# Keys turned in 32x32 blocks by VectorE, and the plain transfers issued by SyncE, in a hybrid mLSTM / gMLP / memory-attention layer with a hierarchical MoE

## The reference

```python
mem_k = (rmsnorm(mem_prompt) @ w_k)        # prompt: 256 memory tokens, 4 heads of 256; also an output
# sample: the keys come from cache_mem_k (256 tokens, 4 heads of 256)
z = rmsnorm(x) @ w_in                      # ONE projection: mLSTM q,k,v,o,i,f; gMLP u,v; memory queries mq; gates
qm = mq_raw.reshape(B, L, MEM_HEADS, MEM_HEAD_DIM)
sc = jnp.einsum('blhd,bmhd->bhlm', qm, mem_k).astype(f32) * (MEM_HEAD_DIM ** -0.5)
a = jax.nn.softmax(sc, axis=-1).astype(x.dtype)
att = jnp.einsum('bhlm,bmhd->blhd', a, mem_v).reshape(B, L, MEM_WIDTH)
# then three gated branches, w_out, the MoE (32 experts), the final norm
```

## Time and profile before

| | |
|---|---|
| median of 3 runs | 845.39 us (845.02 to 845.53) |
| the profiled execution, its own time | 845.18 us |
| its span in the trace | 843.4 us |
| granted TensorE clock, as a share of full speed | 0.995 |
| busy share of PE, DVE, ACT, POOL | 98%, 70%, 56%, 11% |

### The profile page before, as it was taken

One profiled execution on the slowest core, in us unless ns is written; L12 is line 12 of the kernel. 1 busy time (PEld: TensorE's weight loads), 2 busy tenths in 40 slices (PEclk: granted clock), 3 DMA queues, 4 the chain that ended last, 5 costly groups with the idle time before them and its releaser, 6 DMA issues. The chain is left out here.

```text
span 843.4 us, 12205 instructions
## 1 busy us (share of the span) xinstructions
PE 826.6 (98%) x4776; PEld 735.4 (87%) x4776; DVE 588.2 (70%) x820; ACT 469.7 (56%) x622; POOL 94.3 (11%) x163
## 2 busy tenths in 40 slices
PE   7999999999999999999999999999999999999994
PEld 7979999988989998899999999878888888888883
DVE  5665487773455457695565556778889989889893
ACT  5655487753433234554334336656868768677763
POOL 3103101040010010000000010010004102210410
PEclk9999999999999999999999999999999999999998
DMA  9658533335543436345436457579999999999960
GB/s 283 211 174 295 166 113 113 113 118 158 184 138 128 161 125 192 120 151 162 148 110 217 150 207 249 207 264 409 395 358 348 363 391 381 357 353 406 363 247 18
DMA packets 96097, 190.78 MB, mean 226 GB/s; under 512 B 5892, under 2 KB 60448, under 8 KB 95904
## 3 DMA queue, kind: packets, MB, share of 16 engines
q1 hardware_dynamic: 90288, 172.52, 58.9%
q0 software_dynamic: 4944, 15.75, 5.4%
q10 hardware_dynamic: 800, 1.66, 0.6%
HBM read 180.65 MB, written 10.03 MB: 226 GB/s over the span
## 5 line engine op out<-in xcount | busy, mean ns | idle before, releaser
L1492 DVE TENSOR_TENSOR w_r<-arena,w_r 128x2048 fp32r<-128x2048 f32 x96 | 216.9, 2285 | 27.7 <-ACT w_r L1088 27.7
L1483 DVE TENSOR_TENSOR unit_r<-arena,unit_r 128x2048 fp32r<-128x2048 f32 x63 | 145.0, 2302 | 128.7 <-ACT unit_r L1077 128.6
L632 PE MATMUL pj<-xn_r,unit_r 128*128 128x320 f32 x1536 | 233.9, 311 | 0.0
L632 PEld LDWEIGHTS pj<-xn_r,unit_r 128*128 128x128 f32 x1536 | 225.6, 188 | 3.7 <-issue 3.0
L979 PE MATMUL pj<-w_r,xg 128*128 128x512 f32 x768 | 191.0, 398 | 0.5 <-DVE xg L1476 0.4
L1088 ACT ACTIVATE w_r<-arena 128x2048 fp32r<-128x2048 f32 x96 | 180.4, 1910 | 2.9 <-DMA arena<-in_w_exp_down 2.1
L979 PEld LDWEIGHTS pj<-w_r,xg 128*128 128x128 f32 x768 | 141.8, 188 | 31.4 <-DVE xg L1476 0.8
L1077 ACT ACTIVATE unit_r<-arena 128x2048 fp32r<-128x2048 f32 x63 | 120.2, 1908 | 42.3 <-PE pj L632 23.6
L1008 PE MATMUL pj<-w_r,hidT 128*128 128x512 f32 x384 | 93.3, 392 | 0.6 <-ACT hidT L1339 0.6
L1008 PEld LDWEIGHTS pj<-w_r,hidT 128*128 128x128 f32 x384 | 71.8, 188 | 17.0 <-issue 0.8
L632 PE MATMUL pj<-br_r,unit_r 128*128 128x320 f32 x384 | 59.6, 311 | 0.0
(11 more groups left out here) (375 smaller groups left out, 834.0 us busy)
## 6 DMA issues: line engine op xcount, KB each, us to landing
arena<-in_w_in SPq DMA_DIRECT2D x40, 1024.0 KB, 5.3
arena<-in_w_exp_gate SPq DMA_DIRECT2D x64, 512.0 KB, 4.7
arena<-in_w_exp_up SPq DMA_DIRECT2D x64, 512.0 KB, 6.5
arena<-in_w_exp_down SPq DMA_DIRECT2D x64, 512.0 KB, 5.6
arena<-in_w_mem_v SPq DMA_DIRECT2D x4, 1024.0 KB, 5.2
arena<-in_w_br_mem SPq DMA_DIRECT2D x4, 1024.0 KB, 4.9
arena<-in_w_br_mlstm SPq DMA_DIRECT2D x4, 1024.0 KB, 5.0
arena<-in_w_br_gmlp SPq DMA_DIRECT2D x4, 1024.0 KB, 5.0
```

What stands on the lines that cost most here:

```text
L632: last = mm(bank_of(s)[0:out_rows, 0:out_cols], l, r, start=k == 0, stop=k == len(pairs) - 1)
L1483: v.tensor_tensor(unit_r[n % RING][:, 1, :], raw_unit[unit_slot(n)], unit_r[n % RING][:, 0, :], ALU.subtract).then_inc(u_lo, 1)
L1492: v.tensor_tensor(w_r[u % NS][:, 1, :], raw_w[u % NS], w_r[u % NS][:, 0, :], ALU.subtract).then_inc(m_lo, 1)
```

## The change

Keys. Each head's keys are loaded in a form in which transposing 32x32 blocks is the whole turn: partition 32a + i, place (b, j, t) holds key 32b + i, dim 64a + 2j + t. It takes four transfers of 32 partitions for each head and source, each run of 64 floats (256 bytes). The prompt's keys are read back for this from the output `mem_k_prompt`, once it is written. DVE's 32x32 transpose (`v.transpose`, two for each head) writes `kmT` directly; PE's eight `ka` steps and their PSUM banks are gone. A key dim then stands at partition 32a + j, half t, so the query columns must be in the same order: for the units of `mq`, ACT and DVE read the raw unit with a step of two floats and write even columns, then odd columns (`turned`, `unit_part`, `raw_columns`).

Transfers. All that POOL issued, other than the indirect gathers and scatters, is now issued by SP, between the unit loads. Each stands behind a named unit's load.

```diff
-    ka = lambda h: (step("ka", h, 0), step("ka", h, 1))
+    ka = lambda h: (step("ka", h, 0, ring=None, eng=None), step("ka", h, 1, ring=None, eng=None))
...
-        cmk = take(2, 2, HD)
+        cmk = take(2, 2 * HD)
...
+        memk_b = at(B0, H, 2 * HD)
...
+        def turned(n):
+            return UNITS[n][0] == "w_in" and MQ0 <= UNITS[n][1] < GATE0
+        def unit_part(n, part):
+            w = unit_r[n % RING][:, part, :]
+            return w.rearrange("p (k t q) -> p k t q", t=2, q=128) if turned(n) else w
+        def raw_columns(n):
+            w = raw_unit[unit_slot(n)]
+            return w.rearrange("p (k q t) -> p k t q", t=2, q=128) if turned(n) else w
...
+            def load_key_blocks(dst, keys, signal):
+                for a in range(4):
+                    sp.dma_start(dst[32 * a:32 * a + 32, :].rearrange("i (b d) -> i b d", d=64),
+                                 keys.rearrange("(b i) (a d) -> a i b d", i=32, d=64)[a]).then_inc(signal, 16)
...
+            def spread_gate_rows():
+                sp.wait_ge(s_g4, 1)
+                sp.dma_start(spread_rows, rb[0:H, :]).then_inc(s_rbw, 16)
+                sp.wait_ge(s_rbw, 16)
+                sp.dma_start(rbb[:, :, :].rearrange("p h t -> p (h t)"), spread_rows.rearrange("h t -> (h t)").partition_broadcast(128)).then_inc(s_rbb, 16)
...
             for n, (name, col, *part) in enumerate(UNITS):
                 if n == 3:
                     ...
+                    load_gate_weights()
...
+                if n == 6:
+                    sp.dma_start(ws[:, :, :], I["gmlp_w_s"][0].rearrange("g t s -> t g s")).then_inc(s_ws, 16)
+                elif n in (8, 9):
+                    load_cached_keys(n - 8)
+                    load_cache_v(n - 8)
+                elif n == 10:
+                    spread_gate_rows()
+                elif n == 11:
+                    store_memory()
+                elif n == 13:
+                    sp.wait_ge(s_memout, 64)
+                    load_prompt_keys(0)
+                    load_prompt_keys(1)
+                elif n in (16, 18):
+                    sp.wait_ge(s_kmT, n - 14)
+                    load_cached_keys(n // 2 - 6)
+                    load_prompt_keys(n // 2 - 6)
...
+                elif n == 23:
+                    sp.wait_ge(*done("av", 3, 1))
+                    load_state(0)
+                    load_state(1)
...
             for u in range(2, NU):
                 load_unit(0, u)
+                if u == 3:
+                    state_operands_back()
+                elif u == 18:
+                    sp.wait_ge(s_n1row, 1)
+                    sp.dma_start(O["mlstm_n_prompt"]...)
...
-                    pe.wait_ge(*done("ka", h, which))
+                    pe.wait_ge(s_kmT, 2 * h + which + 1)
...
-                af(unit_r[n % RING][:, 0, :], raw_unit[unit_slot(n)], ACT.Copy).then_inc(u_hi, 1)
+                af(unit_part(n, 0), raw_columns(n), ACT.Copy).then_inc(u_hi, 1)
...
-                    v.tensor_copy(kmT[:, h % 2, which, :, :], b.rearrange("p (a m) -> p a m", m=NMEM)).then_inc(free, 1)
+                    dve.wait_ge(s_keys[h % 2], 128 * (h // 2 + 1))
+                    if h >= 2:
+                        dve.wait_ge(*done("sc", h - 2, which))
+                    src = memk_b[:, h, :] if which == 0 else cmk[:, h % 2, :]
+                    v.transpose(kmT[:, h % 2, which, :, :].rearrange("p t (b i) -> p t b i", i=32), src.rearrange("p (b j t) -> p t b j", j=32, t=2)).then_inc(s_kmT, 1)
...
                 elif kind == "attention_done":
                     pool.wait_ge(s_memout, 64)
                     pool.wait_ge(*done("av", 3, 1))
-                    load_state(0)
-                    load_state(1)
                     pool.wait_ge(s_xnl, 3)
                     pair_samples(pair_v, xn_r)
-                    load_router()
```

More of the change, by code:

```diff
@@ new lines, in spread_gate_rows, with store_memory @@
+            def spread_gate_rows():
[3 more added lines that the diff above has]
+                sp.dma_start(rbb[:, :, :].rearrange("p h t -> p (h t)"), spread_rows.rearrange("h t -> (h t)").partition_broadcast(128)).then_inc(s_rbb, 16)
+            def store_memory():
+                sp.wait_ge(s_g3, 1)
+                sp.dma_start(O["mlstm_m_prompt"][0, 0, :].rearrange("(h a) -> h a", a=1), rows[0:H, R_MM, TP - 1:TP]).then_inc(s_mout, 16)
+                sp.dma_start(O["mlstm_m_sample"][0, 0, :].rearrange("(h a) -> h a", a=1), rows[0:H, R_MM, T - 1:T]).then_inc(s_mout, 16)
+                sp.wait_ge(*done("memv", 1, 1, 1))
+                for name, src in (("mem_k_prompt", memk), ("mem_v_prompt", memv)):
+                    for i in range(2):
+                        sp.dma_start(O[name][0, 0, i * 128:(i + 1) * 128].rearrange("p h d -> p (h d)"), src[:, i, :]).then_inc(s_memout, 16)
@@ new lines, in store_conv, with keep_keys, keep_values @@
+            def store_conv():
+                sp.wait_ge(*done("cvT", 1))
+                for i, name in enumerate(("mlstm_conv_prompt", "mlstm_conv_sample")):
+                    sp.dma_start(O[name][0, 0].rearrange("j (c p) -> (j c) p", p=128), cvs[:, i, :]).then_inc(s_cvout, 16)
+            def keep_keys(h):
+                sp.wait_ge(*done("kt", h, 0))
+                sp.dma_start(k_store[:, h, :], kw[:, 0:2, :].rearrange("p i d -> p (i d)")).then_inc(s_kst, 16)
+            def keep_values():
+                sp.wait_ge(*done("v", 1, 1, 1))
+                sp.wait_ge(s_vones, 1)
+                sp.dma_start(v_store, v_tm[:, 0:2, :, :].rearrange("p i h d -> p (i h d)")).then_inc(s_vst, 16)
@@ new lines, in store_state, with store_normalizer, store_gating_values @@
+            def store_state(h):
+                sp.wait_ge(*done("c1", h, 1, 1))
+                sp.dma_start(O["mlstm_C_sample"][0, 0, h].rearrange("(k p) e -> p k e", p=128), c1s[:, :, 0:HD]).then_inc(s_s1out, 16)
+            def store_normalizer():
+                sp.wait_ge(*done("nT"))
+                sp.dma_start(O["mlstm_n_sample"][0, 0].rearrange("h (k p) -> (h k) p", p=128), nrow[0:2 * H, :]).then_inc(s_nout, 16)
+            def store_gating_values():
+                sp.wait_ge(s_gnd, 3)
+                sp.dma_start(O["gmlp_v_sample"][0, 0], gv_tm[0:64, 2, :]).then_inc(s_gvout, 16)
@@ new lines, in state_operands_back @@
+            def state_operands_back():
+                sp.wait_ge(*done("gate", 1, 7))
+                sp.wait_ge(*done("br", 0, 7))
+                sp.wait_ge(*done("hT", 2, 1))
+                sp.wait_ge(s_spm, 8)
+                sp.wait_ge(s_kst, 16 * H)
+                sp.wait_ge(s_vst, 16)
+                for k in range(2):
+                    sp.dma_start(at(STATE_K[k], 4 * HD), k_store[:, 2 * k:2 * k + 2, :].rearrange("p h d -> p (h d)")).then_inc(s_kvin, 16)
+                c0 = 0
+                for off_, heads in STATE_V:
+                    n = heads * (HD + 2)
+                    sp.dma_start(at(off_, n), v_store[:, c0:c0 + n]).then_inc(s_kvin, 16)
+                    c0 += n
@@ L792, in _ @@
                         last = tr(b[:, g * 128:g * 128 + 128], ws[:, g, :], ident[:, :])
[L793 to L802, removed]
                 elif kind == "sc":
@@ L1969, in state_operands_back @@
[L1969 to L1990, removed]
-            pool.dma_start(fb[:, :], I["mlstm_f_b"][0, :].rearrange("(h a) -> h a", a=1)).then_inc(s_par, 16)
@@ L1992, in _ @@
[L1992 to L2007 removed]
+            g.memset(wif, 0.0).then_inc(s_const, 1)
```

119 lines of the change are left out of this document (48 added, 71 removed).

## The result

The changed kernel takes 840.99 us (median of 6 runs, 839.76 to 842.06), the kernel before beside it 845.25 us (6 runs, 844.96 to 846.6). The ratio is 0.9944, interval 0.9934 to 0.9954: 0.56% faster, 4.3 us in the medians. The forecast was 842.8, that is 2.6 us faster. The profiled execution took 841.19 us with a span of 839.4, against 845.18 and 843.4 before; between these two the difference is 4.0 us.

The account below looks back on a forecast made before the run. PE, busy for 98% of the span, was taken as the bound. Terms -3.2 - 0.65 - 0.25 + 1.5 = -2.6 us gave 842.8 us against 845.4, with a range of 841.1 to 846.6.

Parts of the forecast that it names:

- The products: PE at the keys: all 32 turning products go, 0.79 us for each of four heads, -3.2 us.
- `pair_v`: PE's wait for POOL's pairing of sample tokens: goes without POOL's two state loads (1.44 us) ahead of it, -0.65 us.
- Unit 3: PE's early wait for unit 3's split: goes, as gate-column loads cost 2.1 us of queue time either way, -0.25 us.
- Gates' rows: SP's write held behind unit 10's load: DVE begins 2.2 us later, PE waits for unit 10, +1.5 us.
- The queue behind it: SP's queue after the gates' rows: units 11 and 12 still arrive in time, unit 12 with 2 us to spare, 0.
- that rival: A queue taken for hidden is not, likeliest the stores ahead of unit 12: 847.5 us or more, chance 0.11.
- the long trip: Rival at gates' rows: PE waits 3 to 5 us for unit 10; 844.3 to 846.3 us; chance 0.25 with early gate columns.
- the cached keys and values, costed at nothing: Cached keys for heads 0 and 1 issued at 53 to 62 us, each behind a unit's load: no cost.
- Splits with a step of two: `mq` unit splits on ACT and DVE: unchanged 1.9 and 2.3 us; rival of half speed gives 850.8 us, chance 0.07.
- "Every other engine and queue is hidden behind PE": Premise from busy shares and PE's stops between 20 us and the experts: only PE's own work and waits count.
- "the trip is free": Rival at gates' rows: the write is not held back, PE never waits for unit 10; -4.1 us, 841.3 us, chance 0.07.

Follow-up runs that it names:

- the run with the pairing first: Kernel before, with POOL pairing the sample tokens ahead of its two state loads; 844.39 us, ratio 0.9978 to the kernel before.
- the run of keys with the pairing first: Kernel before with only the keys' part, all transfers by POOL, and POOL pairing ahead of the two state loads; 842.44 us, ratio 0.9950.
- the run with the write first: Changed kernel with SP writing the gates' rows ahead of unit 10's load and reading them back behind it; 839.02 us, ratio 0.9918 to the kernel before.
- the run with the late ones: Changed kernel with the late plain transfers (outputs, k and v rows, prompt's normalizer) on POOL's queue again; 840.79 us, ratio 0.9950 to the kernel before.

## Why the prediction was wrong, and what of it held

- **The products: -3.2, measured -3.3.** -0.73, -0.86, -0.88 and -0.87 us at the four heads. The transposes took 1.30 us for two with no wait, as assumed, and ended 1.1 us ahead of the scores.
- **`pair_v`: -0.65, measured -0.9.** The mechanism held, and the run with the pairing first shows it alone (-0.8). But the term is not independent of the first one. With the products gone and POOL's order kept, the wait becomes 2.06 us and eats 1.4 of the 3.3. I compared POOL's 1.4 us with a wait of 0.65 us, but did not shift PE by the keys' gain first. What the moved state loads are worth once the keys have changed is 2.0 us, read off the run of keys with the pairing first.
- **Unit 3: -0.25, measured +1.0 in the profile, but no term of the change.** This was the step that read one execution as a rule. The columns did hold unit 3 back in SP's queue, from 13.2 to 21.8 us, by far more than the 2.1 us that I took for their cost; yet putting them back gained nothing. The wait varies by 1.1 us on its own.
- **Gates' rows: +1.5, measured +1.0** (0.8 of it as the wait). The mechanism was right and the run with the write first shows it; the size was nearly right. The write was seen at 72.1 us where I had 71.4, in a program that stood 1.0 later; the reading back took 4.1 us where I took 4.6. PE's wish for unit 10 had moved with unit 3 as well.
- **The queue behind it: 0, measured 0.** No wait of PE for unit 11 or 12 came; that rival falls, as does the long trip. (Its 847.5 does not follow from its own condition: 8 us of lateness less the 2 to spare is 6, on 842.8.) But the cached keys and values, costed at nothing, did fill a gap in SP's queue ahead of unit 10.
- **Splits with a step of two: 0, measured 0.15 us on ACT** (2.05 against 1.90) and none on DVE (2.29). That rival falls. The Trainium skill's rule on 16-byte lines ("Advanced Engine Details and Errata", "SBUF Cachelines") agrees to within these 8%.
- **The end: no term, measured -1.8.** This is the step that failed. "Every other engine and queue is hidden behind PE" put POOL's transfers at nothing, from the shares of the whole span and PE's waits between 20 us and the experts; the prediction never looked at what stands behind the last instruction of PE. They are not free: the more transfers POOL has issued, the longer the program takes after the last scatter, where nothing hides it. From the last scatter to the end of the span, and the part of it behind the scatter's landing:

| plain transfers issued by POOL | 0 | 2 | 5 | 12 | 19 | 48 | 50 | 78 |
|---|---|---|---|---|---|---|---|---|
| us | 4.2 to 4.5 | 4.2, 4.3 | 4.5 | 4.8 | 5.0 | 6.1 | 6.2 | 6.9 |
| us behind the landing | 0.6 | 0.7 | 0.8 | 1.1 | 1.4 | 2.6 | 2.7 | 3.4 to 3.5 |

(6.2 - 4.4) / 50 is 0.036 us for each. Behind the landing it is (2.7 - 0.6) / 50 = 0.04 up to 50 transfers, and less from there to 78. The table holds all fourteen profiles. The run with 48 small transfers added to the changed kernel shows that the number is the cause, and beside the run with the late ones, that packets and bytes are not. What POOL does in that time no view shows, and it was not tested.

So PE's own path gave -2.2 us (+1.0 +1.0 -3.3 -0.9) in the profile for a forecast of -2.6, and the other 1.8 us came from a place that the prediction did not look at. That -2.2 lies so near to -2.6 is partly luck: unit 3 missed by +1.3, and the other three terms by -0.9 together. My range began at 841.1, which stood for "the trip is free" and for nothing else (the rival itself says 841.3, from the median; 841.1 is from the profiled execution); the median fell below it by 0.1.

The queue rule that I cited (the Trainium skill's "DMA: Bandwidth & Descriptors", "Queues, rings and completion order") is borne out: behind unit 10 the write was seen after 4.9 us, ahead of it after 1.9, and its packets moved among the last of unit 10's.

## What to carry to other kernels

Read the end of the program as a stage of its own: from the last transfer issued to the end of the span nothing is hidden, and here it shrank by 0.036 us for each plain transfer taken from POOL's queue. Before reading a spread between runs as the kernel's own, lay each run's granted clock beside its time. When a change moves PE forward, redo each wait behind it with the new arrival before pricing it: a producer that follows its own chain does not move along, and a wait of 0.65 us became one of 2.06. A short transfer that another engine waits for goes ahead of the bulk load in a queue, not behind it; moving 6 KB ahead of 1 MB took away PE's wait of 0.8 us and gave the fastest kernel of the study.

## What the runs showed of the hardware

- The end of the program grows with the number of transfers that POOL has issued, over the whole program, at some 0.036 us each, whether they carry 16 bytes or 256 KB.
- A transfer of 16 bytes issued by POOL made 32 packets in its queue (1,536 for 48).
- POOL's casts and DVE's unit split (two SBUF operands) slow each other: 3.25 and 2.79 us together, 1.43 and 2.29 when they are not together. In the changed kernel the casts fall beside DVE's L1650, keep their 1.43 us, and DVE pays: 2.40 us for three instructions instead of 1.74. The Trainium skill's "GPSIMD Engine Reference", "Specifications", names this contention with DVE instructions of two SBUF inputs; both pairs agree. No run has the casts with DVE idle.
- DVE's transpose in 32x32 blocks costs what a copy of as many elements from PSUM costs: 1.30 us for two of 128x512, against 1.28.
- In some executions of the same program the granted clock falls to 1.2 GHz for some 3.4 us at about 530 us, in the midst of unbroken work of PE, and costs 1.7 us. What starts it stays open. In another run it fell while PE stood idle for 6.7 us, and PE's first 3.6 us of work behind that wait ran at the lower level.
